# A mixer-and-experts trunk: the first pair's expert rows by one-hot products on TensorE in place of a gather

## What is computed

```python
def hier_moe(h, ...):                       # h = rmsnorm(x, norm_ffn[l]), 512 x 1024
    g_logits = ht @ w_rg + b_rg             # 4 groups; the best one is taken
    e_logits = ...                          # 8 experts of that group; the best two are taken
    w = g_w * top_p / jnp.sum(top_p, axis=-1, keepdims=True)
    ...                                     # tokens are sorted by expert
    def expert_block(args):
        xb, e = args
        return (jax.nn.silu(xb @ w_gate[e]) * (xb @ w_up[e])) @ w_down[e]
    ...                                     # weighted sum back to the tokens, x = x + result
```

## Time and profile before

| | |
|---|---|
| median of 3 runs | 1826.41 us (1824.87 to 1828.58) |
| the profiled execution | 1827.64 us, span 1825.8 us |
| mean granted clock of TensorE | 0.976 |
| TensorE, matmul busy | 1654.2 us, 91% |
| VectorE busy | 596.0 us, 33% |
| ScalarE busy | 411.5 us, 23% |
| GpSimd busy | 199.8 us, 11% |
| HBM read and written | 489.25 MB and 30.47 MB |
| share of TensorE, and of transfers, in the chain that ended last | 31% and 15% |

### The profile page before, as it was taken

How to read it: one execution, slowest core, us unless ns; L and a number is a source line. 1 busy time by engine, 2 the same in 40 slices (tenths; PEclk the granted TensorE clock), 3 DMA queues, 4 the chain that set the end, 5 groups by cost and what they waited for, 6 DMA issues and landing times. The chain is left out here.

```text
span 1825.8 us, 22382 instructions
## 1 busy us (share of the span) xinstructions
PE 1654.2 (91%) x7764; PEld 863.8 (47%) x7764; DVE 596.0 (33%) x1750; ACT 411.5 (23%) x999; POOL 199.8 (11%) x283
## 2 busy tenths in 40 slices
PE   8999999999998778787999999999999978778888
PEld 6666766454443323332367577654543333333333
DVE  4885356334000000000278844553340000000003
ACT  3323555011111111111122254540111111010101
POOL 0012421000100100000000134210001100000000
PEclk9999999999999989999999999999999998999999
DMA  6631101565999999999947111026569999999998
GB/s 171 144 104 47 47 24 47 207 253 189 411 426 428 427 426 426 428 426 428 390 113 198 51 48 47 24 56 240 223 257 413 427 427 427 425 428 426 428 425 344
DMA packets 121907, 496.44 MB, mean 272 GB/s; under 512 B 42036, under 2 KB 78900, under 8 KB 94160
## 3 DMA queue, kind: packets, MB, share of 16 engines
q1 hardware_dynamic: 109584, 472.75, 65.5%
q0 software_dynamic: 8928, 16.52, 2.4%
q10 hardware_dynamic: 3296, 5.84, 0.8%
HBM read 489.25 MB, written 30.47 MB: 285 GB/s over the span
## 5 line engine op out<-in xcount | busy, mean ns | idle before, releaser
L1266 PE MATMUL bank<-arena 128*64 128x512 f32 x2176 | 691.3, 619 | 90.0 <-DMA arena<-in_expert_up 33.6
L1266 PEld LDWEIGHTS bank<-arena 128*64 128x64 f32 x2176 | 228.8, 142 | 353.6 <-issue 353.6
L2239 DVE SCALAR_TENSOR_TENSOR arena<-bank,halves,arena 128x512 f32<-128x512 f32 x32 | 24.0, 750 | 812.9 <-PE bank L1266 812.9
L1266 PE MATMUL bank<-h,arena 128*64 128x512 f32 x320 | 142.2, 621 | 27.1 <-DMA arena<-in_expert_gate 8.7
L1266 PE MATMUL bank<-spare_slot,arena 128*64 128x512 f32 x320 | 133.4, 614 | 28.8 <-ACT arena L1669 9.2
L891 PE MATMUL bank<-arena,hT 128*128 128x256 f32 (+1 forms) x512 | 119.3, 390 | 4.1 <-DMA arena<-in_w_in 3.2
L1266 PE MATMUL bank<-hT,arena 128*64 128x512 f32 x256 | 120.7, 627 | 0.0
L1159 PE MATMUL bank<-arena,hT 128*128 128x512 f32 x256 | 115.0, 597 | 0.0
L891 PEld LDWEIGHTS bank<-arena,hT 128*128 128x128 f32 x512 | 96.8, 192 | 20.5 <-issue 3.4
L1667 ACT ACT_TABLE_LOAD x32 | 41.1, 1283 | 255.8 <-PE bank L1266 255.8
L915 PE MATMUL bank<-hT,arena 128*128 128x256 f32 x384 | 97.0, 387 | 0.5 <-ACT arena L1510 0.5
(11 more groups left out here) (382 smaller groups left out, 1936.3 us busy)
## 6 DMA issues: line engine op xcount, KB each, us to landing
arena<-in_expert_up SPq DMA_DIRECT2D x48, 2048.0 KB, 36.2
arena<-in_expert_gate SPq DMA_DIRECT2D x44, 2048.0 KB, 36.6
arena<-in_expert_down SPq DMA_DIRECT2D x44, 2048.0 KB, 38.5
arena<-in_w_in SPq DMA_DIRECT2D x26, 1024.0 KB, 5.6
spare_slot<-in_expert_gate SPq DMA_DIRECT2D x8, 2048.0 KB, 30.3
h<-in_expert_gate SPq DMA_DIRECT2D x8, 2048.0 KB, 31.8
hT<-in_expert_up SPq DMA_DIRECT2D x8, 2048.0 KB, 41.1
spare_slot<-in_expert_down SPq DMA_DIRECT2D x8, 2048.0 KB, 38.1
```

Source lines behind the costliest of these rows:

```text
L1266: r = pe.matmul(dst[CAP * e:CAP * e + CAP, :], moving[:, k, CAP * e:CAP * e + CAP], w, start=(k == 0), stop=(k == n - 1))
L2239: STT(hid, bank[:, 3, :], slot_root, hid, ALU.mult, ALU.mult).then_inc(act_ready, 1)
```

## The change

1. TensorE makes pair 0's turned rows itself. For each tile VectorE computes first_slot = 128 A_ + B_ for a token's two experts, and first_hot, a 128x128 tile that has 1 where a token belongs in a slot of pair 0 and 0 elsewhere (places of other pairs give numbers over 127). first_rows multiplies 128 columns of x, taken with a stride of 8, by first_hot, and adds up over the tiles in PSUM banks 0 and 1. open_rows opens the sums there with a product by zeros. Tiles 0 to 2 stand before and behind prefix, tile 3 behind the last tabulate. keep_at_work goes.
2. slot_hot and pair_hot are made by GpSimd (slots_of), into one buffer in place of two. It waits for VectorE's new semaphore placed, and from tile 1 on for the product of the tile before.
3. VectorE no longer waits for table_mm in assign; it makes the counts of rounds first, then multiplies by the gain (gain_rows) with the table's two operations in between. table_ready comes last.
4. Pair 0 is still gathered, for the root column alone; TensorE no longer waits for it, VectorE does, and ScalarE's Silu waits for the root (xg_ready).
5. SP's waits before loads 8 and 9 go.
6. TensorE enters the experts' semaphores before project_out_and_route, and in each pair's gate waits for one xg_ready fewer; in the loop the root's copy stands behind both multiplications.

```diff
-        slot_hot = view(107, 2, 2, P)
-        pair_hot = view(109, 2, 2, P)
+        slot_hot = view(107, 2, P)
+        pair_hot = view(108, 2, P)
+        first_hot = view(109, NT, P)
+        zeros_h = view(106.25, P // 2).bitcast(BF16)
...
+                def slots_of(t):
+
+                    pool.wait_ge(placed, t + 1)
+                    if t:
+                        pool.wait_ge(table_mm, t)
+                    for k in range(2):
+                        pool.tensor_scalar(slot_hot[:, k, :], iota_f[:, :], place[:, B_, t, k:k + 1], None, ALU.is_equal)\
+                            .then_inc(slots_ready, 1)
+                        pool.tensor_scalar(pair_hot[:, k, :], iota_f[:, :], place[:, A_, t, k:k + 1], row_f[:, t, k:k + 1],
+                                           ALU.is_equal, ALU.mult).then_inc(slots_ready, 1)
+
+                pool.wait_ge(merged, KD)
+                pool.memset(zeros_h, 0.0).then_inc(zeros_ready, 1)
+                for t in range(NT):
+                    slots_of(t)
                 pool.wait_ge(table_ready, 1)
                 pool.wait_ge(x_out, 32 * NT)
                 gather(table[:, 1, 0:1])
...
                 load(7, 1)
                 sp.wait_ge(out_mm, 2 * NT)
                 leave(sp, left_mix)
-                sp.wait_ge(x_out, 32 * NT)
                 load(8, 1)
-                sp.wait_ge(rows_in, 16)
                 load(9, 1)
                 sp.wait_ge(rounds_ready, 1)
...
                     if t >= 2:
-                        pe.wait_ge(slots_ready, 4 * (t - 1))
+                        pe.wait_ge(placed, t - 1)
...
 
                 for k in range(2):
                     pe.wait_ge(slots_ready, 4 * t + 2 * k + 2)
-                    r = pe.matmul(bank[:, 2, 0:P], slot_hot[:, t % 2, k, :], pair_hot[:, t % 2, k, :],
+                    r = pe.matmul(bank[:, 3, 0:P], slot_hot[:, k, :], pair_hot[:, k, :],
                                   start=(t == 0 and k == 0), stop=(t == NT - 1 and k == 1))
                 r.then_inc(table_mm, 1)
 
-            def keep_at_work(n):
-
-                for i in range(n):
-                    pe.matmul(bank[:, 3, :], ident[:, :], x[:, i % NT, 0:512], start=True, stop=True)
+            def open_rows():
+
+                pe.wait_ge(zeros_ready, 1)
+                pe.wait_ge(x_mixed, 2 * NT)
+                for c in range(2):
+                    pe.matmul(bank[:, c, :], zeros_h, ones_h[:, :].unsqueeze(1).broadcast_to([P, 4, P]), start=True, stop=False)
+
+            def first_rows(c, *tiles):
+
+                for t in tiles:
+                    pe.wait_ge(hot_ready, t + 1)
+                    for k in range(4):
+                        r = pe.matmul(bank[:, c, P * k:P * k + P], x[:, t, 4 * c + k:D:KD], first_hot[:, t, :],
+                                      start=False, stop=(t == NT - 1 and k == 3))
+                    if t == NT - 1:
+                        r.then_inc(xt_done, 1)
...
                         tabulate(t - 1)
                 t = NT - 1
                 turn_x(t, 1)
+                open_rows()
                 logits(t, 1)
-                keep_at_work(KEEP[0])
+                first_rows(0, 0, 1, 2)
                 prefix(t)
-                keep_at_work(KEEP[1])
+                first_rows(1, 0, 1, 2)
                 tabulate(t)
-                keep_at_work(KEEP[2])
+                first_rows(0, t)
+                first_rows(1, t)
...
                     wait_reg(pe, xg_ready, it * 3 + 2)
-                    matrix(bank[:, 2, :], 6 * pp, gate_free, it * 3 + 4)
+                    matrix(bank[:, 2, :], 6 * pp, gate_free, it * 3 + 3)
...
-                pe.wait_ge(rows_in, 16)
-                turn_rows()
                 pe.wait_ge(rounds_ready, 1)
...
                 merge()
+                enter(pe, exp_clear, l)
                 project_out_and_route()
                 leave(pe, left_mix)
-                enter(pe, exp_clear, l)
...
                 with act.Fori(0, nb * PAIRS) as it:
+                    wait_reg(act, xg_ready, it * 3 + 4)
                     wait_reg(act, gate_free, it * 2 + 2)
                     act.activation(hid, bank[:, 2, :], ACT.Silu, scale=slot_root).then_inc(silu_done, 1)
...
                     do(TS(pl(T0_), pl(FIRST), -0.5, (NE - 0.5) / 2, ALU.mult, ALU.add))
                     do(TS(pl(T0_), pl(T0_), ROUND, None, ALU.add))
-                    if t >= 2:
-                        dve.wait_ge(table_mm, t - 1)
                     dve.wait_ge(prefix_mm, t + 1)
...
                     do(TS(pl(ROUND_), pl(T1_), ROUND, None, ALU.subtract))
-                    link(STT(pl(B_), pl(ROUND_), -float(CAP), pl(H64), ALU.mult, ALU.add))
-                    do(STT(pl(A_), pl(ROUND_), float(PAIRS), pl(PAIR), ALU.mult, ALU.add))
-                    for k in range(2):
-                        TS(slot_hot[:, t % 2, k, :], iota_f[:, :], place[:, B_, t, k:k + 1], None, ALU.is_equal)\
-                            .then_inc(slots_ready, 1)
-                        TS(pair_hot[:, t % 2, k, :], iota_f[:, :], place[:, A_, t, k:k + 1], row_f[:, t, k:k + 1],
-                           ALU.is_equal, ALU.mult).then_inc(slots_ready, 1)
+                    n = link(STT(pl(B_), pl(ROUND_), -float(CAP), pl(H64), ALU.mult, ALU.add))
+                    link(STT(pl(A_), pl(ROUND_), float(PAIRS), pl(PAIR), ALU.mult, ALU.add))
+                    link.sync()
+                    dve.sem_inc(placed, 1)
+                    do(STT(first_slot[:, t, :], pl(A_), float(P), pl(B_), ALU.mult, ALU.add))
+                    do(TS(first_hot[:, t, :], iota_f[:, :], first_slot[:, t, 0:1], None, ALU.is_equal))
+                    STT(first_hot[:, t, :], iota_f[:, :], first_slot[:, t, 1:2], first_hot[:, t, :], ALU.is_equal, ALU.add)\
+                        .then_inc(hot_ready, 1)
+
+                def gain_rows(q):
+                    TT(xg[:, 4 * q:4 * q + 4, :], bank[:, q, :].rearrange("p (k c) -> p k c", k=4),
+                       bc(g_ffn[:, 4 * q:4 * q + 4], P), ALU.mult).then_inc(xg_ready, 1)
...
                 choose(NT - 1)
                 assign(NT - 1)
                 do(dve.tensor_reduce(cnt[:, 8:9], bank[:, 6 + (NT - 1) % 2, 96:96 + NE], AX.X, ALU.max))
-                dve.wait_ge(table_mm, NT)
-                do(TS(table[:, 0, :].rearrange("p (h w v) -> p h w v", h=4, w=4),
-                      bank[:, 2, 0:P].rearrange("p (h v w) -> p h w v", h=4, w=4), float(EMPTY), None, ALU.add))
-                TS(table[:, 1, :], table[:, 0, :], 1, None, ALU.logical_shift_right).then_inc(table_ready, 1)
                 do(TS(cnt[:, 0:8], thr[:, :], cnt[:, 8:9], None, ALU.is_lt))
                 do(dve.tensor_reduce(cnt[:, 9:10], cnt[:, 0:8], AX.X, ALU.add))
                 link(TS(cnt[:, 10:11], cnt[:, 9:10], 1.0, None, ALU.add))
+                do(TS(cnt[:, 11:12], cnt[:, 9:10], float(PAIRS), None, ALU.mult))
+                dve.tensor_copy(rounds[:, :], cnt[:, 10:12]).then_inc(rounds_ready, 1)
+                dve.sem_inc(xg_ready, 1)
+                dve.wait_ge(xt_done, 1)
+                gain_rows(0)
+                dve.wait_ge(table_mm, NT)
+                do(TS(table[:, 0, :].rearrange("p (h w v) -> p h w v", h=4, w=4),
+                      bank[:, 3, 0:P].rearrange("p (h v w) -> p h w v", h=4, w=4), float(EMPTY), None, ALU.add))
+                dve.wait_ge(xt_done, 2)
+                gain_rows(1)
+                TS(table[:, 1, :], table[:, 0, :], 1, None, ALU.logical_shift_right).then_inc(table_ready, 1)
                 link(TS(cnt[:, 12:13], cnt[:, 9:10], float(PAIRS), float(PAIRS - 1), ALU.mult, ALU.add))
-                do(TS(cnt[:, 11:12], cnt[:, 9:10], float(PAIRS), None, ALU.mult))
-                dve.sem_inc(xg_ready, 1)
-                dve.tensor_copy(rounds[:, :], cnt[:, 10:12]).then_inc(rounds_ready, 1)
...
                 def root_rows():
                     dve.tensor_copy(slot_root, xrow[:, D:D + 1]).then_inc(xg_ready, 1)
 
-                def gain_rows(q):
-                    TT(xg[:, 4 * q:4 * q + 4, :], bank[:, q, :].rearrange("p (k c) -> p k c", k=4),
-                       bc(g_ffn[:, 4 * q:4 * q + 4], P), ALU.mult).then_inc(xg_ready, 1)
-
-                for q in range(2):
-                    dve.wait_ge(xt_done, q + 1)
-                    gain_rows(q)
-                    if q == 0:
-                        root_rows()
+                dve.wait_ge(rows_in, 16)
+                root_rows()
 
                 def gated(it):
                     wait_reg(dve, silu_done, it + 1)
@@ -2243,9 +2274,8 @@
                     for q in range(2):
                         wait_reg(dve, xt_done, it * 2 + (q + 3))
                         gain_rows(q)
-                        if q == 0:
-                            wait_reg(dve, act_ready, it + 1)
-                            root_rows()
+                    wait_reg(dve, act_ready, it + 1)
+                    root_rows()
```

More of the change, by code:

```diff
@@ L70 @@
 NRING = 4
-KEEP = (4, 3, 6)
 PLAIN = 2
```

(6 more changed lines are left out.)

## The result

The changed kernel takes 1839.11 us (median of 6 runs, 1837.52 to 1840.98) against 1828.32 for the kernel before, measured beside it: a ratio of 1.0067, 95% interval 1.0056 to 1.0077. That is 10.8 us more, where 6.8 less were forecast. The profiled execution took 1837.52 us, span 1835.8, so 10.0 more span than before.

The account below looks back on a forecast made before the run. Weight transfers at 425 to 429 GB/s were taken as the bound. Pair 0 4.4 us earlier, less 1.0 given back, gave 3.4 per layer, 6.8 in two: 1819.6 us forecast, range 1816.8 to 1825 (own range 1817 to 1822.8).

Parts of the forecast that it names:

- Part 1: Pair 0's rows by one-hot products in place of gather, landing and turning: pair 0 starts 4.4 us earlier.
- So 12 products cost 2.7 us: TensorE's one-hot products for tiles 0 to 2: two passes each, 0.11 us a pass; 24 products in all.
- They hide ... and cost nothing: The 24 products of tiles 0 to 2 hide behind VectorE's choice and placement; uncovered they would be 5.3 us.
- 0.53 to pair 0: Step from the end of VectorE's gain multiplication to pair 0's start, taken as 0.53 us.
- I take 0.3: Each of GpSimd's four slot-table operations per tile costs 0.3 us; slots complete at 1345.8.
- the formula of the rival: GpSimd operations of g us, stalling tiles 0 and 1: gain per layer 9.4 - 12g; slower by GpSimd, chance 0.07.
- the comparing row: Profile row of a one-input 128x128 compare-and-fill pass at 0.29 us, used to price GpSimd's operations.
- Part 2: Gathers off pair 0's path: gather 0's root covered by some 2 us, gather 1's rows by 2.4 us.
- Stores of x ... may land as late as 1348: Stores sharing the engines with load 8 may land by 1348; the gather doesn't want them before 1350.
- gather 1 lands in 5.4 us today: Pair 1's gather takes 5.4 us, so lands at 1360.3, before pair 1's turning at 1362.7.
- Part 3: Removing SP's waits before loads 8 and 9: worth only load 9's rest; 1.0 of the 4.4 us given back.
- The clock: Rival: TensorE starts pair 0 at 1.2 GHz, half a gate product takes 3.5 us more, no change; chance 0.03.

Follow-up runs that it names:

- e1: Changed kernel with one-hot products reading 128 neighbouring columns of x instead of every eighth, pair 0's features in wrong order: 1827.3 us, ratio 1.0000.
- e2: Changed kernel with the slot tables made on VectorE again, strided products kept: 1836.6 us, ratio 1.0053.
- e3: Changed kernel with both neighbouring columns (pair 0's features in wrong order) and slot tables on VectorE: 1823.3 us, ratio 0.9975.
- e4: Changed kernel with SP's two waits before loads 8 and 9 put back: 1842.9 us, ratio 1.0085.
- e6: e3 with pair 0's weights laid out to suit neighbouring columns, but by a slip pair 8 got pair 0's weights: 1828.1 us, ratio 1.0003.
- e9: e3 made whole: only pair 0's weight loads take the layout for neighbouring columns, everything computed: 1824.5 us, ratio 0.9983.
- e7: e3 with TensorE's drain moved ahead of the last tile's products and its register loads between their halves: 1825.3 us, ratio 0.9983.
- e5: Kernel before with only SP's two waits before loads 8 and 9 removed: 1838.2 us, ratio 1.0053.
- e10: Kernel before with only SP's second wait removed, load 8 still waiting for the stores of x: 1835.5 us, ratio 1.0045.
- e12: e11 with the slot tables on GpSimd as in the change: 1823.7 us, ratio 0.9980.
- e11: e9 with drain and register loads moved, table first, load 8 behind x stores, pair 0's root by one-hot products, no gather 0: 1820.5 us, ratio 0.9963.

## Why the prediction was wrong

What bounds the kernel and where the change acts were right. Four sizes were wrong, each of them too small, and the first of them made another engine the one that sets pair 0's start.

1. **Part 1, "So 12 products cost 2.7 us" and "They hide ... and cost nothing".** This is the step that failed. The 0.11 us a pass came from the table's product, whose weights are neighbouring columns. The change reads every eighth column, and such a pass takes 0.24 us. Tiles 0 to 2 took 11.6 us, not 5.3, and pushed the prefix 2.1 us back; tile 3's took 4.0, not 1.8. TensorE became the engine in series that VectorE and GpSimd were thought to be. The last tile's table product came 4.7 us later than forecast against turn_x, and from there to pair 0 it took 6.4 us, not 2.9: together the 8.2 us between the forecast start (12.4 after turn_x) and the measured one (20.6). The trace before held a warning that the prediction doesn't use: turn_rows (L1249) reads with the same stride, and its weight load took 193 ns, against 141 for turn_x (L1170), which turns neighbouring columns. e1 settles it: without the stride the whole loss is gone.

```profile
L1249 PEld LDWEIGHTS bank<-ident,arena 128*128 128x128 f32 x256 | 31.0, 193 | 26.4 <-issue 24.3 <-DMA arena<-x_rows,table 2.1
L1170 PEld LDWEIGHTS bank<-ident,x 128*128 128x128 f32 x64 | 7.4, 141 | 5.3 <-issue 4.2 <-DVE x L2101 1.1
```

2. **Part 1, "0.53 to pair 0".** I took the distance from VectorE's multiplication to pair 0 from the trace. There, TensorE's drain and register loads had run while it waited for rows. With the products right ahead of pair 0 they cost 2.0 to 2.3 us after the last product, in every run that leaves them there (e1, e2, e3, e4, e6, e9); e7 shows what they are.
3. **Part 1, "I take 0.3".** GpSimd's compare took 0.61 us and its compare with multiply 0.84, outside both bounds (0.29 and 0.45). By the formula of the rival a mean of 0.73 gives a gain of 0.6 us a layer, so by that term alone the forecast would have been "no change". e1 came out at 1.0000, but not by that term alone: its start is 1.5 us earlier than before, and the clock in layer 1 and pair 1's rows in layer 0 took that back. In the changed kernel the term was hidden at the last tile. The Trainium skill, GPSIMD Engine Reference, on elementwise cost, gives 12 cycles an element for data-dependent branching, by which the prediction's estimate was 1.28 us: neither that rule nor the comparing row that I set against it gave the size. Beside VectorE's one-hot operations GpSimd's second operation took 0.91 us in place of 0.79 (1352.44); in the tile before, at 1337.44, it took 0.79 and VectorE's took 0.45 in place of 0.35. That agrees in kind with the exclusion that the Trainium skill, SBUF — State Buffer, describes in its section on the two sides; its size here was 0.1 us.
4. **Part 2, "Stores of x ... may land as late as 1348" and "gather 1 lands in 5.4 us today".** Behind the two loads the last store needed 12.1 us, where the forecast allowed 9.5 (1348 less its issue at 1338.51). That was harmless here. Gather 0's cover held: VectorE copied the root at 1366.04, and ScalarE wanted it at 1369.43. Gather 1's didn't. It was issued at 1366.99, 0.7 us behind load 10, where it had been 3.1 us ahead of load 10 before, and TensorE had its rows after 11.0 us, not 5.4. So pair 1 stood 1.8 us in layer 1. No run separates what held this gather. **Part 3** took the removal of SP's waits for a small gain by itself. Alone it is a loss of 10.9 us (e5), and of 8 for its second half (e10): the waits kept two big loads out of the way of a small store and a gather. The forecast saw them only as idle transfer time. One reading there is off as well: in the window from 1351 to 1363 the view of transfers (4.14 MB) counts 0.26 MB in GpSimd's queue and 3.87 in the other, so 1.77 MB were load 10's and later, not 1.51. At 427 GB/s that is 0.6 us more given back than reckoned, 1.1 or more in place of 0.5 or more, and inside the bounds of that term.
5. **Rivals.** The clock did fall, in layer 0, where TensorE idled for 2.2 us ahead of pair 0: 1.7 us for half a gate product, half of the price that I gave. It had a chance of 0.03, and e1, e3, e4, e5, e6, e9, e10 and e12 show it too, in one layer or in both. The stalls of tiles 0 and 1, about 0.26 us each, are half of what the formula gives for g = 0.73 (0.5). No rival had TensorE as the engine that is late.

**The sum as measured.** From the same point of layer 0's stream to that of layer 1 (issue of load 2: 904.6 us apart before, 367.45 to 1272.05, and 910.4 after, 366.43 to 1276.82) the first layer lost 5.8 us, which is 0.5 of stalls, 3.8 of start, 1.7 of clock, less a little that the stream gave back. Layer 1 lost the rest of 11.0, 5.2: 0.5 and 3.8, and the 1.8 of pair 1's rows less what was given back. The profiled execution had begun 1.0 us ahead by then, which leaves the 10.0 of its span. How the remainder of under 1 us a layer splits is open, and so is how much of the 1.0 that Part 3 gave back is in it.

That the mechanism works at all is shown by e11: the start 3.4 us and load 14 3.4 us earlier a layer, and 7.1 us of the whole. It has the strides, the tail, GpSimd's part and gather 0 removed, the table first and the wait for the stores kept; with GpSimd's part left in (e12) 3.9 us of the gain stay. That 7.1 is near the 6.8 of the forecast is chance: the start gained 3.4 and not 4.4, and none of it was given back.

## What to carry to other kernels

Before an operation's time is taken from a row, compare the access pattern and not the shape alone: here a stride in the weights of a float32 product more than doubled the pass. When a long wait is removed from an engine's path, list all that the engine did in that wait (drains, register loads); with the wait gone it may stand in series, as here behind the last product. And a wait that seems to leave transfers idle may keep a small store or a gather, on which the path hangs, from landing behind megabytes: test its removal alone.

## What the runs showed of the hardware

- A weight load of 128 columns in float32 took 192 ns with neighbouring columns and 335 with a stride of 8 elements; the passes followed each other by 0.11 and 0.24 us (e1 against the changed kernel), at a granted clock of 1.00 in both.
- GpSimd's tensor_scalar over 128x128 float32 with per-partition operands took 0.61 us with one operation, 0.84 with two; VectorE's took 0.28 and 0.34 in the kernel before.
- An 8 KB store took about 12 us to land when issued behind two loads of 2 MB (12.2 in e5, 11.6 in e3), 2.5 us without them (the kernel before); a gather of 128 rows 7.3 us to TensorE's start in place of 3.9 (e10).
- A drain and two register loads on TensorE took 2.0 to 2.3 us in series behind the last product. Moved between the products, the loads left a gap of 1.09 us in e7, and of 0.66 in e11 and 0.20 in e12 at the same place (layer 1).
- TensorE's clock was granted at 1.00 from 1300 to 1362 in the changed kernel, and from 1336 to 1353 before. For some microseconds at pair 0's start it was at the lower level, 1.2 GHz (16 products in 4.2 to 5.4 us, not 3.65), behind gaps of 2.0 to 4.3 us on TensorE: in both layers of e4, e5 and e10, and in one layer of the changed kernel, e1, e3, e6 and e9. In the other layer of these five, and in both of e2, the same gap of 2.0 to 2.3 us passed without it. In layer 0 of e12 it fell with no gap longer than 0.9 us ahead of it (0.59 granted from 445 to 446).
